# Layer 1's sliding-window scores as six single-pass products on split operands, in place of two fp32 products

## The chip, the cores and the metric

The kernel runs on one core of a Trainium2 chip, in one launch. The metric is the device time of that core in microseconds (us). TensorE is called PE here, its weight loads PEld, VectorE DVE, ScalarE ACT, GpSimd POOL, and SyncE, which issues most DMAs, SP.

## The reference, cut to what matters

A two-layer trunk over 1024 tokens of width 1024, all in float32. Layer 0 mixes by retention and by dilated attention, layer 1 by sliding-window attention with 16 query heads, 4 key heads and one sink logit per head; each layer ends in a squared-ReLU MLP of width 4096. The change touches layer 1's scores alone:

```python
def swa_mixer(h, positions, w_qkv, b_qkv, w_out, q_gain, k_gain, sinks):
    ...
    q = rope(rmsnorm(to_heads(q, SWA_Q_HEADS), q_gain), positions, ROPE_DIMS, ROPE_THETA)
    k = rope(rmsnorm(to_heads(k, SWA_KV_HEADS), k_gain), positions, ROPE_DIMS, ROPE_THETA)
    ...
    o, _ = banded_attn(q, k, v, SWA_WINDOW - 1, sinks.reshape(SWA_KV_HEADS, g))
    ...
# banded_attn, window 128, heads of 64
s = jnp.einsum('bhgnqd,bhnkd->bhgnqk', qb, kb) * (d ** -0.5)
...
p = jnp.exp(s - m)
...
o = jnp.einsum('bhgnqk,bhnkd->bhgnqd', p, vb) / den
```

## The kernel before, in words

Activations lie transposed in SBUF as two tensors each, a rounded part and a remainder (`hT_hi`, `hT_lo`), both of the type float32r, and so do the weights (`W_hi`, `W_lo`). A product of the big matrices is three single-pass products: hi with hi, hi with lo, lo with hi (`three`, lines 350 to 352). The attention's own products are in plain float32, which the chip runs as two instructions for each product.

Layer 1's attention is a software pipeline of 36 slots, written out by hand for each engine (`s_slots`). There are four groups of heads, each with one key head and four query heads, and eight blocks of 128 tokens (a = 0 to 7) in a group, so 32 slots carry a projection of one block (8 steps of three products with 384 columns, line 350). A slot has two halves (j = 0 and 1), and each half handles one unit: two of the four query heads for one block. For unit n of a half, PE does in this order: two steps of the projection; the scores of unit n (line 405); the transposes of the probabilities of unit n-1 (line 422); one step; the product with V of unit n-2 (line 434); one step. At the end of the second half PE transposes the normed queries and keys of the next block into the PSUM tile `qt` (line 441). There is one `qt`.

The other engines follow the same slots in an order of their own. ACT: squares of the queries and keys for their norms (line 652), copies `qt` out into `qT` and `kT` (lines 686, 688), copies the transposed probabilities out (line 664), takes the exponentials of a unit (lines 676, 679), and in four of each eight slots rounds a piece of the next weights (line 620). DVE: adds the bias to the projection, which frees its PSUM tile (line 1105), scales a finished unit by its denominator (lines 1071 to 1075), sums the squares (line 1006), masks the scores and finds their maxima (lines 1049 to 1057), norms and rotates queries and keys (lines 1015 to 1032). POOL: gain (line 1225), the reciprocal root (lines 1239, 1241), and the remainder of the weights' piece (line 1209). The key transposes serve both row halves: `heads_T` writes two query heads one under the other (64 partitions each) and the key head twice, so that the scores of one head use rows 0 to 63 of PE's array and those of the other rows 64 to 127. The two heads' scores go to two PSUM banks.

What holds the order together are counting semaphores: `qkt_ready` tells PE that `qT` and `kT` of a block are written, `s_done` tells DVE of finished scores, `sm_ready` tells ACT and PE that the maxima are found, `p_ready` that the exponentials are, `qt_done` that `qt` is filled, `gemm_evac` that a projection's PSUM tile is free.

Of the kernel before, what the change touches and what calls it, by code (L numbers as in the profile page):

```python
# [29 lines left out]
def hybrid_trunk(nc, x_in, positions, norm_mix, norm_mlp, w_up, w_down, w_in, w_out0, gn_gain, dq_gain, dk_gain,  # L30
                 w_qkv, b_qkv, w_out1, sq_gain, sk_gain, sinks, out, x_spill):
    f32, f32r, i32 = mybir.dt.float32, mybir.dt.float32r, mybir.dt.int32
    ALU = mybir.AluOpType
    ACT = mybir.ActivationFunctionType
    AX = mybir.AxisListType

    P = 128
    S, D = x_in.shape[1], x_in.shape[2]
    T = S // P
# [3 lines left out]
    HD = 64  # L43
# [36 lines left out]
    with ctx:  # L80
# [6 lines left out]
        def sem(name):  # L87
            return ctx.enter_context(nc.semaphore(name))
# [42 lines left out]
        off = [A0]  # L131

        def at(name, shape, dt=f32):
            t = nc.alloc_sbuf_tensor_at(name, shape, dt, offset=off[0])
            off[0] += 4 * int(math.prod(shape[1:]))
            assert off[0] <= nc.sbuf_usable_end, (name, off[0])
            return t
# [2 lines left out]
        G = at("G", [P, RING, W])  # L140
        V = at("V", [P, T, 2 * HD])
        QK = at("QK", [P, 2, W])
        kT = at("kT", [P, S])
        qT = at("qT", [P, 2, 2 * P])
        Pm = at("Pm", [P, 2, 1024])
        pT = at("pT", [P, 2, 1024])
        rsT = at("rsT", [P, P])
        rR = at("rR", [HD, 2, RV])
        rsg = at("rsg", [P, 2, RV])
        re = at("re", [P, 2, RV])  # L150
        rQK = at("rQK", [P, 2, 2 * HD])
        rqT = at("rqT", [HD, 3, P])
        off[0] = A0
        a_hi, a_lo = [0, 0], [0, 0]
        a_hi[0], a_lo[0] = at("a_hi0", [P, 2, S], f32r), at("a_lo0", [P, 2, S], f32r)
# [21 lines left out]
        sc = ps("sc", [P, 1024])  # L177
        tp = ps("tp", [P, 1024])
        o_ps = ps("o_ps", [P, 512])
        qt = ps("qt", [P, 512])  # L180
# [23 lines left out]
        r_exp, r_qk, r_qt, r_qtev, r_st, r_sT, r_R, r_o, r_var, r_rstd, r_x = [  # L204
            sem(n) for n in ("r_exp", "r_qk", "r_qt", "r_qtev", "r_st", "r_sT", "r_R", "r_o", "r_var",
                             "r_rstd", "r_x")]
        h_sq, h_gain, h_ss, h_rstd, qk_ready, qt_done, qkt_ready, v_ready = [
            sem(n) for n in ("h_sq", "h_gain", "h_ss", "h_rstd", "qk_ready", "qt_done", "qkt_ready", "v_ready")]
        s_done, sm_ready, p_ready, tp_done, pt_ready, pv_done, o_evac = [
            sem(n) for n in ("s_done", "sm_ready", "p_ready", "tp_done", "pt_ready", "pv_done", "o_evac")]  # L210
        u_done, u_evac, a_sq, a_hi_done, a_ready, d_done, d_evac = [
# [133 lines left out]
        def _(pe):  # L345
            mm = nc.tensor.matmul
# [40 lines left out]
            def scores(kind, n, u0):  # L387
                g, a, j = unit(n)
                if j == 0:
                    pe.wait_ge(qkt_ready, (u0 + n) // 2 + 1)  # L390
                if u0 + n >= 1:
                    pe.wait_ge(sm_ready, u0 + n)
                if kind == "D" and n == 0 and u0 > 0:

                    pe.wait_ge(r_x, u0 // 2)
                if kind == "D":
                    r = slice(HD * j, HD * (j + 1))
                    for c in range(0, (a + 1) * P, 512):
                        e = min(c + 512, (a + 1) * P)
                        last = mm(sc[:, c:e], qT[r, a % 2, 0:P], kT[r, c:e], start=True, stop=True)  # L400
                else:
                    k0 = max(a - 1, 0) * P
                    for e in range(2):
                        r = slice(HD * e, HD * (e + 1))
                        last = mm(sc[:, e * 512:e * 512 + (a + 1) * P - k0], qT[r, a % 2, j * P:(j + 1) * P],
                                  kT[r, k0:(a + 1) * P], start=True, stop=True)
                last.then_inc(s_done, 1)

            def blocks(kind, a):
# [28 lines left out]
            def heads_T(kind, t, a0):  # L438
                pe.wait_ge(qk_ready, a0 + t + 1)
                for m in range(2 if kind == "D" else 3):  # L440
                    last = nc.tensor.transpose(qt[:, m * P:(m + 1) * P], QK[:, t % 2, m * P:(m + 1) * P], ident[:, :])
                last.then_inc(qt_done, 1)
# [169 lines left out]
        def _(act):  # L612
            A = nc.scalar.activation
# [69 lines left out]
            def heads_T_copy(kind, t, a0):  # L683
                m = 1 if kind == "D" else 2
                act.wait_ge(qt_done, a0 + t)
                A(qT[:, (t - 1) % 2, 0:m * P], qt[:, 0:m * P], ACT.Copy)
                c = (t - 1) % T * P
                A(kT[:, c:c + P], qt[:, m * P:(m + 1) * P], ACT.Copy).then_inc(qkt_ready, 1)

            def dr_slots():  # L690
                for s in range(DR_SLOTS):
# [113 lines left out]
            for h in range(RH):  # L805
# [3 lines left out]
                last = A(cdec[:, h:h + 1], dq[:, P + 2:P + 3], ACT.Exp, scale=LG[h])  # L809
# [50 lines left out]
        def _(dve):  # L860
            E = nc.vector
# [146 lines left out]
            def prep(kind, t, a0):  # L1008

                H = 4 if kind == "D" else 5  # L1010
                q = QK[:, t % 2, 0:H * HD].rearrange("p (h d) -> p h d", h=H)
                dve.wait_ge(h_gain, a0 + t + 1)
                dve.wait_ge(h_rstd, a0 + t + 1)
                rb = rstd[:, 0:H].rearrange("p (h o) -> p h o", o=1).to_broadcast([P, H, HD])
                step.did(E.tensor_tensor(q, q, rb, ALU.mult))
                A3 = ropeA[:, 0:H * 16].rearrange("p (h s d) -> p h s d", h=H, s=2)
                B3 = ropeB[:, 0:H * 16].rearrange("p (h s d) -> p h s d", h=H, s=2)
                q4 = q[:, :, 0:2 * HALF_D].rearrange("p h (s d) -> p h s d", s=2)
                cc = cosD[:, t % T, :].rearrange("p (m s d) -> p m s d", m=1, s=1).to_broadcast([P, H, 2, HALF_D])
                sn = sinD[:, t % T, :].rearrange("p (m d) -> p m d", m=1).to_broadcast([P, H, HALF_D])  # L1020
                step.wait()
                step.did(E.tensor_tensor(A3, q4, cc, ALU.mult))
                step.did(E.scalar_tensor_tensor(B3[:, :, 0, :], q4[:, :, 1, :], -1.0, sn, ALU.mult, ALU.mult))
                step.did(E.tensor_tensor(B3[:, :, 1, :], q4[:, :, 0, :], sn, ALU.mult))
                step.wait()
                if kind == "D":
                    E.tensor_tensor(q4, A3, B3, ALU.add).then_inc(qk_ready, 1)
                else:
                    step.did(E.tensor_tensor(q4, A3, B3, ALU.add))
                    step.wait()  # L1030

                    E.tensor_copy(QK[:, t % 2, 5 * HD:6 * HD], QK[:, t % 2, 4 * HD:5 * HD]).then_inc(qk_ready, 1)
# [66 lines left out]
            def bias_G(t):  # L1099
                if t - 1 >= RING:  # L1100
                    dve.wait_ge(v_ready, A_S + t - RING)
                if (t - 1) % T == 0:
# [2 lines left out]
                E.tensor_tensor(G[:, (t - 1) % RING, :], gp[:, (t - 1) % 2, 0:W], biasS[:, (t - 1) // T % 2, :],  # L1105
                                ALU.add).then_inc(gemm_evac, 1)

            def s_slots():
                units = NG * 2 * T
                for t in range(S_SLOTS):  # L1110
                    for j in range(2):
                        n = 2 * t + j - 4
                        if j == 0 and 1 <= t <= NG * T:
                            bias_G(t)
                        if 0 <= n - 3 < units:
                            outputs("S", n - 3, U_S, 0)
                        if j == 0 and 0 <= t - 1 < units // 2:
                            sums("S", t - 1, A_S)
                        if 0 <= n < units:
                            maxima("S", n, U_S, 0)  # L1120
                        if j == 0 and 0 <= t - 1 < units // 2:
                            prep("S", t - 1, A_S)

            def out_proj(n0, k, m, full):
                lo_T(0, k, 0)
# [270 lines left out]
```

## Time and profile before

| | us |
|---|---|
| three runs, median (lowest to highest) | 2614.23 (2612.29 to 2614.32) |
| the profiled execution, its own time | 2612.44 |
| its span, first to last instruction | 2610.7 |
| layer 1's score products, first to last start | 1491.0 to 1761.5 |
| mean granted TensorE clock | 0.981 of full speed |

PE is the busy engine nearly everywhere. The stage of the change is the stretch from 1480 to about 1766 us; the other engines are busier there than in most of the kernel. A timeline row gives an instruction's start and its length; PE's instructions are pipelined, so the lengths of neighbours overlap, and the pace is read from start to start. The number behind a row in brackets is how long the engine was idle ahead of it, and what ended that.

### The profile page before, as it was taken

Reading aid. Unit: us, or ns where it says so; the run is one execution under the profiler, and the core shown is the slowest. Engines: PE = TensorE matmul, PEld = TensorE weight load, DVE = VectorE, ACT = ScalarE, POOL = GpSimd, SP = SyncE. Lnnn points to the kernel's source line nnn. Section 1 sums busy time; section 2 is a strip of 40 time slices with the busy share of each in tenths; the row PEclk is TensorE's granted clock in tenths of the full one; section 3 lists DMA queues with packets and bytes.
Section 4 is the critical chain, followed back from the end, with each engine's and each line's share of the span. In section 5 each row is a group of like instructions: output and inputs, shape, how many; then the busy total and the mean of one; then the engine's idle time right before and its main releaser. Section 6 shows DMA issues by size and latency. Waiting matters only on the chain.

```text
span 2610.7 us, 34016 instructions
## 1 busy us (share of the span) xinstructions
PE 2486.2 (95%) x12520; PEld 2080.3 (80%) x12520; DVE 1075.7 (41%) x2591; ACT 739.6 (28%) x1487; POOL 806.7 (31%) x770
## 2 busy tenths in 40 slices
PE   5999999998989999999999799999989999999998
PEld 4787878787968888888887688879978888888886
DVE  7464645454323232323233566662322323232323
ACT  4424343331221212121221355552312121212220
POOL 4223132310333333333332233331133333333331
PEclk9999999998999999999999899998999999999999
DMA  3000000002211111111111200003011111111111
GB/s 115 25 25 25 25 25 25 25 19 80 69 33 49 48 48 48 48 48 48 48 48 43 89 26 25 25 25 103 31 49 49 48 48 48 48 48 48 48 48 65
DMA packets 108200, 120.20 MB, mean 46 GB/s; under 512 B 26048, under 2 KB 94144, under 8 KB 108096
## 3 DMA queue, kind: packets, MB, share of 16 engines
q1 hardware_dynamic: 100720, 103.70, 12.8%
q10 hardware_dynamic: 7376, 15.12, 1.7%
q8 instruction: 64, 1.05, 0.2%
q14 instruction: 40, 0.33, 0.0%
HBM read 110.41 MB, written 8.39 MB: 46 GB/s over the span
## 4 chain that ended last, share of the span: by engine, by line
PE 84%; DVE 8%; POOL 3%; ACT 2%; issue 2%; DMA 0%; POOLq 0%; SPq 0%; ACTq 0%; DVEq 0%
PE gp L350 11%; PE gp L352 10%; PE gp L351 10%; PE sc L350 5%; PE sc L352 4%; PE sc L351 4%; PE tp L351 4%; PE tp L352 4%; PE tp L350 4%; PE o_ps L434 4%; PE sc L400 3%; PE tp L422 2%; PE o_ps L350 2%; PE qt L350 2%; PE qt L351 2%; PE o_ps L352 2%
## 5 line engine op out<-in xcount | busy, mean ns | idle before, releaser
L1209 POOL TENSOR_TENSOR W_lo<-raw,W_hi 128x1024 fp32r<-128x1024 f32 (+2 forms) x200 | 433.7, 2183 | 704.1 <-ACT W_hi L620 704.0
L350 PE MATMUL gp<-W_hi,hT_hi 128*128 128x384 f32 (+1 forms) x1152 | 421.9, 366 | 14.8 <-POOL W_lo L1209 6.7
L352 PE MATMUL gp<-W_hi,hT_lo 128*128 128x384 f32 (+1 forms) x1152 | 384.3, 334 | 0.0
L351 PE MATMUL gp<-W_lo,hT_hi 128*128 128x384 f32 (+1 forms) x1152 | 383.9, 333 | 0.0
L620 ACT ACTIVATE W_hi<-raw 128x1024 fp32r<-128x1024 f32 (+2 forms) x200 | 186.4, 964 | 646.7 <-PE qt L352 559.0
L1148 DVE TENSOR_TENSOR r<-r 128x512 f32<-128x512 f32 x128 | 92.2, 720 | 626.8 <-ACT r L773 626.8
L1295 POOL TENSOR_TENSOR a_lo<-r,a_hi 128x512 fp32r<-128x512 f32 x128 | 166.0, 1298 | 447.5 <-ACT a_hi L775 447.5
L1155 DVE TENSOR_TENSOR X<-tp,X 128x512 f32<-128x512 f32 x256 | 176.8, 692 | 173.8 <-PE tp L352 171.7
L350 PEld LDWEIGHTS gp<-W_hi,hT_hi 128*128 128x128 f32 x1152 | 221.2, 192 | 26.9 <-issue 11.2
L351 PEld LDWEIGHTS gp<-W_lo,hT_hi 128*128 128x128 f32 x1152 | 221.6, 192 | 0.0
L352 PEld LDWEIGHTS gp<-W_hi,hT_lo 128*128 128x128 f32 x1152 | 219.9, 191 | 0.0
L350 PE MATMUL gp<-hT_hi,W_hi 128*128 128x512 f32 x512 | 201.5, 393 | 16.0 <-POOL W_lo L1209 16.0
L350 PE MATMUL tp<-W_hi,a_hi 128*128 128x512 f32 x512 | 204.1, 399 | 11.7 <-POOL W_lo L1209 11.7
L350 PE MATMUL sc<-hT_hi,W_hi 128*128 128x512 f32 x512 | 200.9, 392 | 5.3 <-DVE hT_lo L933 5.3
L351 PE MATMUL tp<-W_lo,a_hi 128*128 128x512 f32 x512 | 204.1, 399 | 0.0
L352 PE MATMUL tp<-W_hi,a_lo 128*128 128x512 f32 x512 | 203.9, 398 | 0.0
L352 PE MATMUL gp<-hT_hi,W_lo 128*128 128x512 f32 x512 | 200.4, 391 | 0.0
L352 PE MATMUL sc<-hT_hi,W_lo 128*128 128x512 f32 x512 | 200.4, 391 | 0.0
L351 PE MATMUL sc<-hT_lo,W_hi 128*128 128x512 f32 x512 | 200.2, 391 | 0.0
L351 PE MATMUL gp<-hT_lo,W_hi 128*128 128x512 f32 x512 | 200.1, 391 | 0.0
L434 PEld LDWEIGHTS o_ps<-V,pT 128*128 128x128 f32 x1056 | 138.5, 196 | 15.8 <-issue 8.7
L434 PE MATMUL o_ps<-V,pT 128*128 128x64 f32 x1056 | 136.8, 274 | 11.1 <-DVE X L1066 7.0
(187 smaller groups left out, 4083.8 us busy)
## 6 DMA issues: line engine op xcount, KB each, us to landing
raw<-in_mlp_w_up SPq DMA_DIRECT2D x64, 512.0 KB, 3.8
raw<-in_mlp_w_down SPq DMA_DIRECT2D x64, 512.0 KB, 3.2
raw<-in_hyb_w_in SPq DMA_DIRECT2D x80, 128.0 KB, 2.5
X<-in_x SPq DMA_DIRECT2D x8, 512.0 KB, 12.0
X<-in_x ACTq DMA_DIRECT2D x8, 512.0 KB, 3.2
raw<-in_swa_w_qkv SPq DMA_DIRECT2D x16, 256.0 KB, 2.7
x_spill<-X ACTq DMA_DIRECT2D x8, 512.0 KB, 2.6
X<-x_spill ACTq DMA_DIRECT2D x8, 512.0 KB, 3.3
```

The source lines that it names most:

```text
L350: mm(o, a[0], b[0], start=first, stop=False)
L351: mm(o, a[0], b[1], start=False, stop=False)
L352: return mm(o, a[1], b[0], start=False, stop=last)
L400: last = mm(sc[:, c:e], qT[r, a % 2, 0:P], kT[r, c:e], start=True, stop=True)
L422: last = nc.tensor.transpose(tp[:, to:to + P], Pm[:, j, c:c + P], ident[:, :])
L434: last = mm(o_ps[:, e * HD:(e + 1) * HD], pT[:, j, to:to + P], V[:, c, v0:v0 + HD], start=(m == 0 or bl[m - 1][3] != e), stop=(m == len(bl ...
L620: A(W_hi[:, slot, n * p:n * (p + 1)], raw[:, p % 2, 0:n], ACT.Copy).then_inc(w_hi, 1)
L1148: E.tensor_tensor(r2[:, ft, :], r2[:, ft, :], r2[:, ft, :], ALU.mult).then_inc(a_sq, 1)
L1155: E.tensor_tensor(x, d_out[(2 * i + nh) % D_BANKS], x, ALU.add).then_inc(d_evac, 1)
L1209: E.tensor_tensor(W_lo[:, slot, c], raw[:, p % 2, 0:n], W_hi[:, slot, c].bitcast(f32), ALU.subtract).then_inc(w_ready, 1)
L1295: E.tensor_tensor(a_lo[par][:, ft, r], r2[:, ft, :], a_hi[par][:, ft, r].bitcast(f32), ALU.subtract).then_inc(a_ready, 1)
```

## The change

Queries and keys of layer 1 are kept as a rounded part and a remainder, each float32r, in memory that the layer-0 tiles had. ACT writes the rounded parts `qS_hi` and `kS_hi` from `qt` where it wrote `qT` and `kT`, and signals the new semaphore `qkt_hi`. DVE gets a new function `heads_T_lo`, two subtractions that write `qS_lo` and `kS_lo`, at the end of each slot, and signals `qkt_ready`. PE's scores of a unit are six products in place of two: hi with hi, hi with lo, lo with hi, and for each of these the two heads in turn, so that neighbouring instructions lie on different row halves. The products of one head accumulate in PSUM. Layer 0 keeps its fp32 scores. The lines of the new file are some 9 to 20 higher than those of the profile.

```diff
--- before.py
+++ after.py
@@ -140,16 +140,23 @@
         G = at("G", [P, RING, W])
         V = at("V", [P, T, 2 * HD])
         QK = at("QK", [P, 2, W])
+        qk0 = off[0]
         kT = at("kT", [P, S])
         qT = at("qT", [P, 2, 2 * P])
         Pm = at("Pm", [P, 2, 1024])
         pT = at("pT", [P, 2, 1024])
+        lo0 = off[0]
         rsT = at("rsT", [P, P])
         rR = at("rR", [HD, 2, RV])
         rsg = at("rsg", [P, 2, RV])
         re = at("re", [P, 2, RV])
         rQK = at("rQK", [P, 2, 2 * HD])
         rqT = at("rqT", [HD, 3, P])
+        off[0] = qk0
+        kS_hi, qS_hi = at("kS_hi", [P, S], f32r), at("qS_hi", [P, 2, 2 * P], f32r)
+        off[0] = lo0
+        kS_lo, qS_lo = at("kS_lo", [P, S], f32r), at("qS_lo", [P, 2, 2 * P], f32r)
+        kS, qS = (kS_hi, kS_lo), (qS_hi, qS_lo)
         off[0] = A0
         a_hi, a_lo = [0, 0], [0, 0]
         a_hi[0], a_lo[0] = at("a_hi0", [P, 2, S], f32r), at("a_lo0", [P, 2, S], f32r)
@@ -204,8 +211,8 @@
         r_exp, r_qk, r_qt, r_qtev, r_st, r_sT, r_R, r_o, r_var, r_rstd, r_x = [
             sem(n) for n in ("r_exp", "r_qk", "r_qt", "r_qtev", "r_st", "r_sT", "r_R", "r_o", "r_var",
                              "r_rstd", "r_x")]
-        h_sq, h_gain, h_ss, h_rstd, qk_ready, qt_done, qkt_ready, v_ready = [
-            sem(n) for n in ("h_sq", "h_gain", "h_ss", "h_rstd", "qk_ready", "qt_done", "qkt_ready", "v_ready")]
+        h_sq, h_gain, h_ss, h_rstd, qk_ready, qt_done, qkt_hi, qkt_ready, v_ready = [
+            sem(n) for n in ("h_sq", "h_gain", "h_ss", "h_rstd", "qk_ready", "qt_done", "qkt_hi", "qkt_ready", "v_ready")]
         s_done, sm_ready, p_ready, tp_done, pt_ready, pv_done, o_evac = [
             sem(n) for n in ("s_done", "sm_ready", "p_ready", "tp_done", "pt_ready", "pv_done", "o_evac")]
         u_done, u_evac, a_sq, a_hi_done, a_ready, d_done, d_evac = [
@@ -400,10 +407,12 @@
                         last = mm(sc[:, c:e], qT[r, a % 2, 0:P], kT[r, c:e], start=True, stop=True)
                 else:
                     k0 = max(a - 1, 0) * P
-                    for e in range(2):
-                        r = slice(HD * e, HD * (e + 1))
-                        last = mm(sc[:, e * 512:e * 512 + (a + 1) * P - k0], qT[r, a % 2, j * P:(j + 1) * P],
-                                  kT[r, k0:(a + 1) * P], start=True, stop=True)
+                    for m, (q, k) in enumerate(((0, 0), (0, 1), (1, 0))):
+                        for e in range(2):
+
+                            r = slice(HD * e, HD * (e + 1))
+                            last = mm(sc[:, e * 512:e * 512 + (a + 1) * P - k0], qS[q][r, a % 2, j * P:(j + 1) * P],
+                                      kS[k][r, k0:(a + 1) * P], start=(m == 0), stop=(m == 2))
                 last.then_inc(s_done, 1)
 
             def blocks(kind, a):
@@ -683,9 +692,13 @@
             def heads_T_copy(kind, t, a0):
                 m = 1 if kind == "D" else 2
                 act.wait_ge(qt_done, a0 + t)
-                A(qT[:, (t - 1) % 2, 0:m * P], qt[:, 0:m * P], ACT.Copy)
                 c = (t - 1) % T * P
-                A(kT[:, c:c + P], qt[:, m * P:(m + 1) * P], ACT.Copy).then_inc(qkt_ready, 1)
+                if kind == "D":
+                    A(qT[:, (t - 1) % 2, 0:m * P], qt[:, 0:m * P], ACT.Copy)
+                    A(kT[:, c:c + P], qt[:, m * P:(m + 1) * P], ACT.Copy).then_inc(qkt_ready, 1)
+                else:
+                    A(qS_hi[:, (t - 1) % 2, :], qt[:, 0:m * P], ACT.Copy)
+                    A(kS_hi[:, c:c + P], qt[:, m * P:(m + 1) * P], ACT.Copy).then_inc(qkt_hi, 1)
 
             def dr_slots():
                 for s in range(DR_SLOTS):
@@ -1105,6 +1118,13 @@
                 E.tensor_tensor(G[:, (t - 1) % RING, :], gp[:, (t - 1) % 2, 0:W], biasS[:, (t - 1) // T % 2, :],
                                 ALU.add).then_inc(gemm_evac, 1)
 
+            def heads_T_lo(t):
+                dve.wait_ge(qkt_hi, t)
+                c = (t - 1) % T * P
+                E.tensor_tensor(qS_lo[:, (t - 1) % 2, :], qt[:, 0:2 * P], qS_hi[:, (t - 1) % 2, :].bitcast(f32), ALU.subtract)
+                E.tensor_tensor(kS_lo[:, c:c + P], qt[:, 2 * P:3 * P], kS_hi[:, c:c + P].bitcast(f32),
+                                ALU.subtract).then_inc(qkt_ready, 1)
+
             def s_slots():
                 units = NG * 2 * T
                 for t in range(S_SLOTS):
@@ -1120,6 +1140,8 @@
                             maxima("S", n, U_S, 0)
                         if j == 0 and 0 <= t - 1 < units // 2:
                             prep("S", t - 1, A_S)
+                        if j == 1 and 0 <= t - 1 < units // 2:
+                            heads_T_lo(t)
 
             def out_proj(n0, k, m, full):
                 lo_T(0, k, 0)
```

PE's order in one half slot, before: `L405` are the score products of the two heads (each is two instructions on the chip), between the projection (`L351`, `L352`) and the transposes of the probabilities (`L422`).

```order
L352 MATMUL gp<-W_hi,hT_lo 128x384
L405 MATMUL sc<-kT,qT 128x256 [waits sm_ready,qkt_ready]
L405 MATMUL sc<-kT,qT 128x256
L422 MATMUL tp<-ident,Pm 128x128 [waits pt_ready,p_ready]
L422 MATMUL tp<-ident,Pm 128x128 x3
```

The same place of PE in the changed kernel, where line 405 is 414, 352 is 359 and 422 is 431.

```order
L359 MATMUL gp<-W_hi,hT_lo 128x384
L414 MATMUL sc<-kS_hi,qS_hi 128x256 [waits sm_ready,qkt_ready]
L414 MATMUL sc<-kS_hi,qS_hi 128x256
L414 MATMUL sc<-kS_lo,qS_hi 128x256 x2
L414 MATMUL sc<-kS_hi,qS_lo 128x256 x2
```

The two products in fp32 became six in float32r, two for each pair of parts; the waits of the first one are the same two.

DVE's order across the end of a slot, before: the maxima of the second half (`L1049` to `L1057`), and then the bias of the next slot (`L1105`).

```order
L1049 ISA Pm,st<-sc,c 128x256 [waits tp_done,s_done]
L1049 ISA st 128x1
L1049 ISA Pm,st<-sc,c 128x256
L1049 ISA st 128x1
L1055 TENSOR_TENSOR st<-st 128x2 [waits dve_step]
L1057 TENSOR_TENSOR st<-st 128x2 [waits dve_step]
L1105 TENSOR_TENSOR G<-gp,nlm 128x384 [waits gemm_done,v_ready]
L1071 TENSOR_TENSOR st<-st 128x2 [waits pv_done]
```

The same place in the changed kernel, where line 1049 is 1062, 1055 and 1057 are 1068 and 1070, 1105 is 1118, 1071 is 1084, and 1124 and 1125 are the new subtractions.

```order
L1062 ISA st 128x1
L1068 TENSOR_TENSOR st<-st 128x2 [waits dve_step]
L1070 TENSOR_TENSOR st<-st 128x2 [waits dve_step]
L1124 TENSOR_TENSOR qS_lo<-qt,qS_hi 128x256 [waits qkt_hi]
L1125 TENSOR_TENSOR kS_lo<-qt,kS_hi 128x128
L1118 TENSOR_TENSOR G<-gp,nlm 128x384 [waits gemm_done,v_ready]
L1084 TENSOR_TENSOR st<-st 128x2 [waits pv_done]
```

The two subtractions stand between the last maxima of a slot and the bias of the next, with a wait for ACT ahead of them.

ACT's order around the same place, before: the exponentials of the slot's second unit (`L676`, `L679`), the copies out of `qt`, and the squares of the next slot.

```order
L676 ACTIVATE st<-st 128x2 [waits sm_ready]
L679 ACTIVATE Pm,st<-Pm,st 128x256 x2
L686 ACTIVATE qT<-qt 128x256 [waits qt_done]
L688 ACTIVATE kT<-qt 128x128
L652 ACTIVATE sq<-G 128x320 [waits h_ss,gemm_evac]
```

In the changed kernel (lines 685, 688, 700, 701, 661):

```order
L685 ACTIVATE st<-st 128x2 [waits sm_ready]
L688 ACTIVATE Pm,st<-Pm,st 128x256 x2
L700 ACTIVATE qS_hi<-qt 128x256 [waits qt_done]
L701 ACTIVATE kS_hi<-qt 128x128
L661 ACTIVATE sq<-G 128x320 [waits h_ss,gemm_evac]
```

ACT's order is the same; only the tiles that it writes have other names and the type float32r.

## Rows read from the trace of the kernel before

**Rows 1.** Page of the profile, part 1: busy time and share of PE

```profile
PE 2486.2 (95%) x12520; PEld 2080.3 (80%) x12520; DVE 1075.7 (41%) x2591; ACT 739.6 (28%) x1487; POOL 806.7 (31%) x770
```

**Rows 2.** Table by stretch of layer 1's attention: window, length, busy per engine, PEclk

```profile
1500.00:1600.00 100.00, 98.93 (x666) 85.18 (x664) 67.80 (x305) 55.77 (x181) 40.70 (x53) 1.00 0.09 23
```

**Rows 3.** Chain of waits, one slot: start, length (us), piece

```profile
1602.32 0.63 PE sc L405 x4
...
1611.06 0.63 PE sc L405 x4
```

**Rows 4.** Line L405 alone, one half slot: duration ns min/median/max

```profile
L405 PE MATMUL sc<-kT,qT x4: 376/428/480, 1602.2 to 1602.6; 64*128 64x256 f32 x4
```

**Rows 5.** Timeline of PE and its weight loads in the same slot: start, length, instruction

```profile
1602.24 0.30 PEld L405 LDWEIGHTS sc<-kT,qT 64*128 64x128 f32 x4 [0.25 <-issue]
1602.25 0.70 PE L405 MATMUL sc<-kT,qT 64*128 64x256 f32 x4
...
1602.88 0.65 PE L422 MATMUL tp<-ident,Pm 128*128 128x128 f32 x4
...
1609.52 0.49 PE L441 MATMUL qt<-ident,QK 128*128 128x128 f32 x3
```

**Rows 6.** Timeline of PE, single-pass products of 256 columns (layer 0's output projection)

```profile
700.05 0.28 PE L350 MATMUL gp<-W_hi,hT_hi 128*128 128x256 f32 x1
700.17 0.28 PE L351 MATMUL gp<-W_lo,hT_hi 128*128 128x256 f32 x1
```

**Rows 7.** Timeline of DVE and ACT, the same slot

```profile
1601.05 0.56 DVE L1105 TENSOR_TENSOR G<-gp,nlm 128x384 f32<-128x384 f32 x1 [1.28 <-PE gp L352]
...
1601.74 0.47 ACT L652 ACTIVATE sq<-G 128x320 f32<-128x320 f32 x1
...
1602.36 0.49 DVE L1006 TENSOR_REDUCE st<-sq 128x5 f32<-128x320 f32 x1 [0.16 <-ACT sq L652]
...
1604.61 0.49 DVE L1015 TENSOR_TENSOR QK<-QK,st 128x320 f32<-128x320 f32 x1 [0.29 <-POOL st L1241]
...
1606.40 0.29 DVE L1075 TENSOR_TENSOR X<-o_ps,st 128x128 f32<-128x128 f32 x1
...
1607.35 0.42 DVE L1049 CUSTOM_DVE_ANT_0 Pm<-sc,c 128x256 f32<-128x256 f32 x1 [0.65 <-PE sc L405]
...
1608.36 0.16 DVE L1057 TENSOR_TENSOR st<-st 128x2 f32<-128x2 f32 x1
...
1609.56 0.19 ACT L679 ACTIVATION_READ_ACCUMULATOR Pm<-Pm,st 128x1 f32 x1
...
1610.05 0.39 ACT L686 ACTIVATE qT<-qt 128x256 f32<-128x256 f32 x1 [0.30 <-PE qt L441]
1610.33 0.27 ACT L688 ACTIVATE kT<-qt 128x128 f32<-128x128 f32 x1
```

**Rows 8.** Timeline of DVE, ACT and POOL, first two slots of a group of heads

```profile
1562.72 1.70 DVE L1032 COPY QK<-QK 128x64 f32<-128x64 f32 x1
...
1564.72 0.29 DVE L1075 TENSOR_TENSOR X<-o_ps,st 128x128 f32<-128x128 f32 x1
...
1573.39 0.71 DVE L1055 TENSOR_TENSOR st<-st 128x2 f32<-128x2 f32 x1
...
1567.18 0.39 ACT L686 ACTIVATE qT<-qt 128x256 f32<-128x256 f32 x1 [0.35 <-PE qt L441]
...
1562.47 1.90 POOL L1209 TENSOR_TENSOR W_lo<-raw,W_hi 128x768 fp32r<-128x768 f32 x1 [1.16 <-ACT W_hi L620]
...
1572.25 1.84 POOL L1209 TENSOR_TENSOR W_lo<-raw,W_hi 128x768 fp32r<-128x768 f32 x1 [1.87 <-ACT W_hi L620]
```

**Rows 9.** Timeline of PE: score products that open the group's first slots

```profile
1559.05 0.49 PE L405 MATMUL sc<-kT,qT 64*128 64x128 f32 x4
...
1568.14 0.70 PE L405 MATMUL sc<-kT,qT 64*128 64x256 f32 x4
...
1576.00 0.70 PE L405 MATMUL sc<-kT,qT 64*128 64x256 f32 x4 [0.16 <-ACT kT L688]
```

## The prediction

> **What bounds the kernel now.** I read four views, in this order. The page's first part says that PE is busy for 95% of the span [rows 1]. The table by stretch says the same of layer 1's attention: PE busy 98.9 of 100 us at full clock (1.00, the 2.4 GHz level), DVE 67.8, ACT 55.8 [rows 2]. The chain of waits shows that this is a real bound and no statistic: from one block's score products to the next, 8.74 us (1602.32 to 1611.06), every piece is PE's [rows 3]. Last I read the timeline of one such slot, for the slack of the engines that PE waits for [rows 5, 7]. PE starts the scores of a block at 1602.25 [rows 5]; ACT has the next block's keys ready at 1610.33 + 0.27 = 1610.60 [rows 7], 8.35 us later, and PE wants them at 8.74. So the slack of this hand-over is 0.39 us. That is the number on which all depends: the change puts two DVE instructions into it.
>
> **What the scores cost on PE.** One half slot has four instructions of 376 to 480 ns [rows 4], 1.71 us in sum, and yet the four take 0.70 us and the transposes start 0.63 us after the first of them [rows 5]. They run in pairs, one head on each row half. 0.63 us is made of a weight load of about 0.1, two passes of 256 columns, and 0.1 until the transposes can begin; so a pass takes some 0.213 us, two clocks for a column. In the new form there are three pairs. A float32r product of 256 columns is followed by the next after 0.12 us [rows 6], one clock for a column and a little, and its weights load behind its neighbour. Three pairs take 0.36 us against 0.43: PE gains 0.07 us in a unit, 0.13 in a slot. The ends around them (0.1 each) stay, since the array is still used in halves there and whole before and after. Bounds for a pair: 0.107 us if it is the bare columns (gain 0.11 a unit), 0.24 us if the two halves' products follow each other at the pace of [rows 6] (loss of 0.29). I take 0.12, because the fp32 pairs of this very place overlap. In units with 128 columns (8 of 64) two short passes of 0.107 stand against three pairs that a weight load of 0.1 may pace: a loss of 0.1 at most, 0.8 us in all, taken as nothing.
>
> A rule that speaks against this: the Trainium skill, "TensorE: Matmul & The Clock Gate", Part 3, The mechanism, says that weight loads overlap running products only when the row groups differ. By it, each pair would wait for its own load, and the unit would cost what the third case below has. The trace does not agree: all four loads of a unit lie within 0.30 us from 1602.24 on [rows 5], so the second pair's weights are in before the first pair has ended, on the same halves.
>
> **What the remainders cost on DVE.** Both read PSUM and SBUF, as the bias does: 0.56 us for 384 columns (L1105), 0.29 for 128 (L1075) [rows 7]. Between them 256 columns come to 0.42. On one engine the second starts some 0.07 us ahead of the first one's end, so the two take 0.36 + 0.29 = 0.65 us. Bounds: 0.5 and 0.8. ACT's copies change only the type they write, for nothing (the bounds are 0.1 us either way). DVE begins 0.15 us after ACT ends (1601.74 + 0.47 to 1602.36 [rows 7]), and PE 0.05 after what it waits for (1575.95 to 1576.00 in another slot, where PE did wait for ACT's keys [rows 9]).
>
> **The first loop, through PE.** From the scores at 0: the transposes of queries and keys at 7.27 (1609.52 - 1602.25 [rows 5]), ACT's copies from 7.80 to 8.35 [rows 7], DVE from 8.50 to 9.15, next scores at 9.20. PE's own gain shortens the first stretch by 0.13: 9.07 us, against 8.74. The added 0.85 us eats the slack of 0.39, and PE idles for the rest.
>
> **The second loop, through DVE and ACT.** DVE works in order, so behind the waiting subtraction stands the bias of the next slot; ahead of it are the maxima, whose exponentials ACT does before it copies `qt`. That closes a ring: subtraction, bias, squares (ACT), sums, root (POOL), norm, scaling, maxima, exponentials (ACT), copies (ACT), subtraction. Its length from the bias at 0, from [rows 7]: squares end at 0.62 + 0.47 and the sums start at 1.24. The norm starts 2.25 after that (1602.36 to 1604.61), 3.49; the scaling 1.79 later (1604.61 to 1606.40), 5.28; the maxima follow at once, 0.21 later, and are done after 1.17 (1607.35 to 1608.52), 6.66. Exponentials: ACT's last instruction starts 1.04 after L1057 ends (1608.52 to 1609.56), and the copies about 0.1 after that, 7.80; they end 0.55 later, DVE comes 0.15 behind, 8.50; two subtractions, 0.6 until the bias can start: 9.10 us. Before, this ring was open: DVE took the bias at 1601.05, ahead of ACT's copies. The two loops tie, and where they lean on each other a little more is lost. I take 9.15 for a plain slot: +0.4.
>
> **The slots with a weights' piece.** Four of eight slots have POOL's L1209, 1.8 to 1.9 us. While it runs, some DVE instructions stand still: the copy L1032 took 1.70 us and ended with it (1562.47 + 1.90), and L1055 took 0.71 and did so too (1572.25 + 1.84) [rows 8]. L1057, of the same kind and size as L1055, takes 0.16 [rows 7]. In most slots these stalls do not meet now, or fall in DVE's idle time; in a ring they count. In the ring's time the first maxima start at 1.67 (the sums at 1.24 and 0.43), end at 2.84, and ACT's exponentials at 3.97; the rounding of weights takes 0.83, so L1209 runs from 4.9 to 6.75, and L1055 of the second half wants 5.49 + 0.80 = 6.29: 0.46 us more, a slot of 9.55. The three slots after a group's first are such. The first one (128 columns, a shorter chain) has L1209 from 4.4 to 6.3; L1032 wants 4.8 and leaves at 6.3; the scaling ends 0.6 later at 6.9. From its end to ACT's copies are 2.17 us now (1565.01 to 1567.18 [rows 8]; PE's product with V, then the transposes), and then 1.40 (0.55, 0.15, 0.65, 0.05) to the next scores: 10.4 us.
>
> The Trainium skill, "SBUF — State Buffer", Who interferes with whom, says that GpSimd and a DVE copy, or a DVE operation with both inputs in SBUF, exclude each other for a whole instruction. The stalls above agree. By it the new subtractions, with one input in PSUM, are not held up, and the sum stays as it is.
>
> **The sum.** A group of eight slots: first 10.4 against 9.09 (1559.05 to 1568.14), second 9.55 against 7.86 (to 1576.00) [rows 9], two at 9.55 and four at 9.15 against 8.74 [rows 3]: 1.3 + 1.7 + 1.6 + 1.6 = 6.2 us. Four groups: 24.8 us. Filling and emptying the pipeline adds one or two hand-overs of 0.85 and loses a slot's worth elsewhere; I leave it at 25. The profiled execution took 2612.4 us, 1.7 of them outside its span of 2610.7, and would take 2637.4. The median of the runs lies 1.8 above it; half of that is noise of three runs, so I say 2638.5.
>
> **The rivals.**
>
> *PE's price alone decides.* DVE is idle for a third of the stage [rows 2], so the subtractions could disappear there. Then the kernel gets the 0.07 us of 56 units: 4 us faster, 0.15%, which is no change as far as this kernel can be measured (0.2%, 5 us, is about the bound). 2610. It decides as soon as the subtractions are done within 0.39 us after ACT's copies; they need 0.85. Against it: the row above, and DVE's idle time lies elsewhere, ahead of the bias and the maxima.
>
> *The ring closes, but POOL's instruction is not met.* First slot 9.1, all others 9.1 to 9.15: 0 + 1.3 + 6 x 0.4 = 3.7 a group, 15 us: 2629. For it: a shift of 0.3 us lets L1055 pass. Against: L1032 in the first slot is met in each of the four groups already, by a row like the first of [rows 8].
>
> *The six products are slower than three pairs of 0.12.* One after another, or each pair behind its own loads, a pair costs 0.21 to 0.24, a unit 0.28 to 0.36 more than in my sum. With 0.21 the PE loop becomes 9.07 + 0.54 = 9.6 us: plain slots +0.9, the middle ones no less, 2 + 4 x 0.9 + 2 x 0.9 + 1.3 = 8.7 a group: 35 us, 2648. With 0.24, 2652. This is also how the change would fail to do what it says. For it: no float32r product on half the rows is in the trace. Against: fp32 overlaps there [rows 4].
>
> **How the numbers follow.** My forecast 0.64, with its own range of 2631 to 2645; the slower products 0.15; no meeting with POOL 0.16; PE's price alone 0.05. The range of eight in ten runs from 2625, which takes in most of the 2629 case, to 2650, which takes in the 35 us case but not its end. Slower by over 0.2% is all but the last case: 0.94; within 0.2% 0.04; faster 0.02.
>
> **What would show it.** Right: in plain slots the starts of the score products stand 9.1 to 9.2 us apart; PE's largest wait in the stage is for `kS_lo` of DVE, some 0.4 us in each slot; DVE's wait for ACT's `kS_hi` becomes its longest, about 2 us in each slot, and its wait of 1.28 us for the projection is gone; ACT's squares wait for the bias; a unit's six products take about 0.6 us with starts in pairs; PE's busy share of the stage falls to some 93%. Wrong: starts of neighbouring score products 0.1 us or more apart everywhere; or PE never waits for DVE there; or L1055 is never longer than 0.2 us; or a granted clock under 1.00 in the stage, which I do not expect of gaps that short.

## The result, and the profile after

Four runs of the changed kernel have a median of 2649.78 us (2649.03 to 2650.53), the kernel before 2613.26 us in the same comparison: ratio 1.0141, 95% interval 1.0128 to 1.0153. The change costs 36.5 us. I had forecast slower, by 25 us to 2638.5; the measured time lies at the very end of my range, and outside the 2631 to 2645 of the case that I held likeliest. As a ratio to the kernel before of its own comparison it lies just past that end: 2650 is 1.0137 of the 2614.23 that I started from, and 1.0141 was measured. The mechanism was there, and one of its terms was about a third of what it should have been.

The page of the changed kernel, span and part 1 (busy time, share, instructions):

```profile
span 2647.6 us, 34336 instructions
PE 2497.7 (94%) x12648; PEld 2094.1 (79%) x12648; DVE 1102.9 (42%) x2655; ACT 739.9 (28%) x1487; POOL 805.7 (30%) x770
```

The span grew by 36.9 us, PE's recorded busy time by 11.5. Between the opening score products of the first and the last unit of layer 1 it grew by 35.8 us (269.9 us before, 305.8 now), ahead of them by 1.5, and behind them it shrank by 0.5.

The same table by stretch as in [rows 2]: window, length, busy time of PE, PEld, DVE, ACT and POOL, granted clock.

```profile
1500.00:1600.00 100.00, 88.39 (x610) 75.85 (x609) 68.93 (x277) 49.81 (x163) 35.05 (x46) 0.98 0.10 26
1600.00:1700.00 100.00, 91.27 (x636) 78.74 (x635) 68.66 (x288) 49.61 (x158) 34.29 (x48) 0.98 0.10 27
```

PE was busy 98.9 us of 100; now it idles for 9 to 12. The waits of the stage in the changed kernel, longest sums first (engine and line waited for, us in total, times, longest):

```profile
POOL QK L1247 <- DVE G L1118: 164.2, 31, 6.4
ACT st L685 <- DVE st L1070: 64.9, 60, 2.9
DVE qS_lo L1124 <- ACT kS_hi L701: 58.2, 32, 2.3
...
ACT sq L661 <- DVE G L1118: 35.7, 31, 1.2
...
PEld sc L414 <- DVE kS_lo L1125: 22.1, 31, 1.7
...
PE o_ps L443 <- DVE X L1088: 18.4, 14, 1.6
PE sc L414 <- DVE kS_lo L1125: 12.1, 30, 1.4
```

DVE waits in all 32 slots for ACT's copies, ACT's squares wait for DVE's bias, and PE waits at the scores in 30 of 32 (12.1 us; its weight loads, PEld, show the same wait as 22.1). Another wait of PE is longer in sum than the one at the scores, 18.4 us in 14 slots, for the scaling of a finished unit (L1088). What that is, the two kinds of slot show.

A plain slot, timeline of the changed kernel (start, length, instruction, idle time ahead and what ended it); these rows answer to [rows 5, 7]:

```profile
1637.46 0.27 ACT L701 ACTIVATE kS_hi<-qt 128x128 fp32r<-128x128 f32 x1
1637.77 0.42 DVE L1124 TENSOR_TENSOR qS_lo<-qt,qS_hi 128x256 fp32r<-128x256 f32 x1 [1.91 <-ACT kS_hi L701]
1638.11 0.28 DVE L1125 TENSOR_TENSOR kS_lo<-qt,kS_hi 128x128 fp32r<-128x128 f32 x1
1638.31 0.55 DVE L1118 TENSOR_TENSOR G<-gp,nlm 128x384 f32<-128x384 f32 x1
1638.89 0.47 ACT L661 ACTIVATE sq<-G 128x320 f32<-128x320 f32 x1 [1.15 <-DVE G L1118]
...
1629.39 0.39 PE L414 MATMUL sc<-kS_hi,qS_hi 64*128 64x256 f32 x2 [0.25 <-DVE kS_lo L1125]
...
1638.45 0.39 PE L414 MATMUL sc<-kS_hi,qS_hi 64*128 64x256 f32 x2 [0.25 <-DVE kS_lo L1125]
1638.67 0.28 PE L414 MATMUL sc<-kS_lo,qS_hi 64*128 64x256 f32 x2
1638.79 0.28 PE L414 MATMUL sc<-kS_hi,qS_lo 64*128 64x256 f32 x2
```

Here the forecast's sum can be read off piece by piece: DVE starts 0.04 us after ACT's copy ends (I had 0.15), the remainders take 0.42 and 0.28 (0.42 and 0.29), PE's scores start 0.06 after them, and the slot is 9.06 us long (1629.39 to 1638.45; I had 9.15, before 8.74). The three pairs start 0.22 and 0.12 us apart: the 0.12 of [rows 6] for a pair, and ahead of the second one the 0.1 that I had taken for a weight load.

A slot with a weights' piece, the same kernel, PE, DVE and POOL:

```profile
1590.35 0.39 PE L414 MATMUL sc<-kS_hi,qS_hi 64*128 64x256 f32 x2 [0.71 <-DVE kS_lo L1125]
...
1597.52 1.08 PE L443 MATMUL o_ps<-V,pT 128*128 128x64 f32 x8 [1.15 <-DVE X L1088]
1600.81 0.39 PE L414 MATMUL sc<-kS_hi,qS_hi 64*128 64x256 f32 x2 [0.26 <-DVE kS_lo L1125]
...
1594.95 0.19 DVE L1045 COPY QK<-QK 128x64 f32<-128x64 f32 x1
1595.06 1.79 DVE L1084 TENSOR_TENSOR st<-st 128x2 f32<-128x2 f32 x1
...
1597.08 0.29 DVE L1088 TENSOR_TENSOR X<-o_ps,st 128x128 f32<-128x128 f32 x1
...
1598.09 0.16 DVE L1068 TENSOR_TENSOR st<-st 128x2 f32<-128x2 f32 x1
...
1595.01 1.82 POOL L1231 TENSOR_TENSOR W_lo<-raw,W_hi 128x768 fp32r<-128x768 f32 x1 [1.47 <-ACT W_hi L629]
```

This slot is 10.46 us long, and so are eight of the twelve second, third and fourth slots of the four groups (the others 9.41 to 11.45); I had 9.55. The instruction that stands still is L1084 (before: L1071), which adds the sink to a unit's denominator: two columns wide, usually 0.15 us, here 1.79. It started 0.05 us after POOL's 1.82 us instruction. The copy ahead of it got through, and the one that I had expected to be held up, L1068, came when POOL was done. Behind L1084 stands the scaling L1088, and for that PE's product with V waits 1.15 us.

In the kernel before the same two instructions meet too, in the third slot of each group, and there DVE is not held up. One of these places (L1071 is now L1084, L1209 is now L1231, L1075 is now L1088):

```profile
1580.11 1.85 POOL L1209 TENSOR_TENSOR W_lo<-raw,W_hi 128x768 fp32r<-128x768 f32 x1 [1.52 <-ACT W_hi L620]
1580.11 0.15 DVE L1071 TENSOR_TENSOR st<-st 128x2 f32<-128x2 f32 x1
...
1580.50 0.29 DVE L1075 TENSOR_TENSOR X<-o_ps,st 128x128 f32<-128x128 f32 x1
```

With the two starts within 0.01 us of each other, L1071 takes its usual 0.15 us; with POOL 0.05 us ahead it takes 1.79. So the price of these slots hangs on 0.05 us in the order of two engines.

### The profile page after: what moved, and what is told of

Read it like the earlier page. It is cut to its first block, busy times and chain, and to the rows that moved or that the text cites. A ratio compares the mean times of both kernels' runs of the same rounds, so it can differ in the third digit from the quotient of the medians.

```text
span 2647.6 us, 34336 instructions
## 1 busy us (share of the span) xinstructions
PE 2497.7 (94%) x12648; PEld 2094.1 (79%) x12648; DVE 1102.9 (42%) x2655; ACT 739.9 (28%) x1487; POOL 805.7 (30%) x770
## 4 chain that ended last, share of the span: by engine, by line
PE 80%; DVE 11%; POOL 3%; issue 3%; ACT 2%; DMA 0%; POOLq 0%; ACTq 0%; DVEq 0%; SPq 0%
PE gp L357 10%; PE gp L359 9%; PE gp L358 9%; PE sc L357 4%; PE sc L359 4%; PE sc L358 4%; PE tp L358 4%; PE tp L357 4%; PE tp L359 4%; PE o_ps L443 4%; PE sc L407 3%; PE qt L357 2%; PE o_ps L357 2%; PE qt L358 2%; PE o_ps L359 2%
## 5 line engine op out<-in xcount | busy, mean ns | idle before, releaser
L1231 POOL TENSOR_TENSOR W_lo<-raw,W_hi 128x1024 fp32r<-128x1024 f32 (+2 forms) x200 | 432.8, 2178 | 704.4 <-ACT W_hi L629 704.3
## 6 DMA issues: line engine op xcount, KB each, us to landing
X<-in_x SPq DMA_DIRECT2D x8, 512.0 KB, 11.5
```

The lines of the kernel that those rows point to most:

```text
L1231: E.tensor_tensor(W_lo[:, slot, c], raw[:, p % 2, 0:n], W_hi[:, slot, c].bitcast(f32), ALU.subtract).then_inc(w_ready, 1)
```

## The experiments

Each comparison has its own runs of the kernel before; times are medians. "Remainders" are the two subtractions L1124 and L1125.

**POOL's long instruction taken away.** The stall was a reading of one trace, so first the cause is removed.

```diff
-                        split_lo(P_S + 4 * (t // T + 1), SPLIT_AT[t % T], t // T % 2, 2 * W)
+                        split_lo(P_S + 4 * (t // T + 1), SPLIT_AT[t % T], t // T % 2, 2 * W, 16)   # 16 columns only
```

> The changed kernel, but POOL computes the weights' remainder for 16 of 768 columns of each piece in layer 1's attention (the rest is left out), so its long instruction is gone there. Theory A (the four slots of a group with a weights' piece are long because DVE stands still while that instruction runs): these slots fall from 10.4 to about 9.1 us, plain slots stay at 9.06, the kernel gets 4 x (1.3 + 3 x 1.4) = 22 us faster than the changed one, about 2628 us. Theory B (those slots are long because the new ring of DVE and ACT also has the rounding of weights in it): they stay near 10.4, and the time near 2650 us.

2625.24 us (2623.14 to 2626.89), a little under the 2628 expected. The third and fourth slots of a group are 9.05 to 9.09 (one 9.22), like the plain ones; the first two are 8.8 and 8.9 (7.9 for the very first). In the trace of this run the score products of the former long slots start at:

```profile
1591.69 0.39 PE L414 MATMUL sc<-kS_hi,qS_hi 64*128 64x256 f32 x2 [0.25 <-DVE kS_lo L1125]
...
1600.76 0.39 PE L414 MATMUL sc<-kS_hi,qS_hi 64*128 64x256 f32 x2 [0.25 <-DVE kS_lo L1125]
...
1609.83 0.39 PE L414 MATMUL sc<-kS_hi,qS_hi 64*128 64x256 f32 x2 [0.25 <-DVE kS_lo L1125]
```

9.07 us each. Theory A holds; the rounding of weights on ACT, which is still there, costs nothing.

**The six products without remainders.**

```diff
-        kS, qS = (kS_hi, kS_lo), (qS_hi, qS_lo)
+        kS, qS = (kS_hi, kS_hi), (qS_hi, qS_hi)
-                    A(kS_hi[:, c:c + P], qt[:, m * P:(m + 1) * P], ACT.Copy).then_inc(qkt_hi, 1)
+                    A(kS_hi[:, c:c + P], qt[:, m * P:(m + 1) * P], ACT.Copy).then_inc(qkt_ready, 1)
```

> The six products as in the changed kernel, but the rounded parts stand in for the remainders (these are left out): DVE's two subtractions are gone, and ACT signals the scores as before. This is PE's price alone. Theory A: six products take 0.55 us until the transposes where the fp32 ones took 0.63, so the stage gains 0.15 us a slot: 4 to 5 us faster than the kernel before, about 2609 us. Theory C (the products themselves are the loss): 2640 us or more.

2612.48 us, ratio 1.0000 (0.9990 to 1.0009): no loss, and no gain of 4 us either. Plain slots are 8.59 us, 0.16 shorter as forecast. But the third slot of each group is 9.53 where it was 8.75. DVE and POOL in it:

```profile
1580.64 1.79 DVE L1084 TENSOR_TENSOR st<-st 128x2 f32<-128x2 f32 x1
...
1583.10 1.08 PE L443 MATMUL o_ps<-V,pT 128*128 128x64 f32 x8 [0.71 <-DVE X L1088]
...
1580.58 1.83 POOL L1229 TENSOR_TENSOR W_lo<-raw,W_hi 128x768 fp32r<-128x768 f32 x1 [1.46 <-ACT W_hi L629]
```

L1084 comes 0.06 us behind POOL's start, where in the kernel before the two started together and it passed. A faster PE shifted two engines against each other by 0.06 us, and one such meeting in each group eats all but 0.1 us of what PE won in the other slots (69.33 us a group against 69.45).

**Both at once: PE's price with nothing in its way.** The two edits above together, and POOL's cut alone in the kernel before.

> The six products with the rounded parts in the remainders' place and no subtraction (the remainders are left out), and POOL's instruction on the weights cut to 16 columns. PE's price with nothing in its way: each slot 0.15 us shorter than in the kernel before with the same cut (2607.3 us), 8.60 where that has 8.75, so about 4.5 us less, 2603 us. If the six products bring nothing on the whole, 2607 us.

> The kernel before, with POOL's remainder of the weights cut to 16 of 768 columns of each piece in layer 1's attention (the rest is left out). Before, the stalls behind POOL's long instruction meet only the first two slots of a group: 1 us there, 4 to 6 us in all, about 2608 us. Set against the same cut in the changed kernel (2625 us) this gives what the change costs with POOL out of the way: theory A says 17 us, and that 20 of the 36 us are stalls that the old order did not meet.

2605.13 us (ratio 0.9964, 0.9950 to 0.9978) against 2607.30 (0.9978, 0.9969 to 0.9988). The times alone don't tell the two apart; the slots do. Score products of two neighbouring plain slots, first kernel and then second:

```profile
1599.62 0.62 PE L414 MATMUL sc<-kS_hi,qS_hi 64*128 64x256 f32 x6
...
1608.21 0.62 PE L414 MATMUL sc<-kS_hi,qS_hi 64*128 64x256 f32 x6
```

```profile
1600.10 0.70 PE L405 MATMUL sc<-kT,qT 64*128 64x256 f32 x4
...
1608.85 0.70 PE L405 MATMUL sc<-kT,qT 64*128 64x256 f32 x4
```

8.59 against 8.75. Over the stage, 261.0 against 264.5 us: the six products gain 3.5 us, near my 4. The second run says more: with POOL's instruction gone, the change costs 2625.24 - 2607.30 = 17.9 us, so of the 36.3 us between the kernels the stalls behind it are about 18 (I had expected 20).

**The remainders without the products.** Two fp32 products as before, and the subtractions at their place, with the waits of the changed kernel.

```diff
+                        if j == 1 and 0 <= t - 1 < units // 2:
+                            heads_T_lo(t)      # results unused; scores from qT and kT, L405 as it was
```

> The kernel before with its two fp32 products, plus the two subtractions of the changed kernel at the same place and with the same waits (their results are not used). Theory A: the loss is the subtractions' place, so this kernel has all of it and lacks PE's small gain: plain slots about 9.2, long ones about 10.4, 2650 to 2655 us. Theory C: near the kernel before, 2613 us.

2648.68 us (ratio 1.0135, 1.0118 to 1.0152), which is the changed kernel's time within the noise. Plain slots 9.15, long ones 10.46. With the runs on PE's price this settles it: the loss is the subtractions, and the products are innocent.

**Does the place on DVE matter?** The same subtractions, behind the bias of the next slot.

```diff
                         if j == 0 and 1 <= t <= NG * T:
                             bias_G(t)
+                        if j == 0 and 0 <= t - 2 < units // 2:
+                            heads_T_lo(t - 1)
...
-                        if j == 1 and 0 <= t - 1 < units // 2:
-                            heads_T_lo(t)
```

> The changed kernel with the two subtractions moved behind the bias of the next slot on DVE, nothing else. Theory A: the ring through the bias is open again, so POOL's root and the norms come 0.5 us or more earlier and the stalls behind POOL's instruction are partly met elsewhere; plain slots stay at 9.05 to 9.2, since PE still waits for the remainders; long slots fall to 9 to 10. Between 2632 and 2643 us. A rival (it is DVE's added work of 0.65 us a slot, wherever it stands) expects no change, 2650 us.

2632.07 us (ratio 1.0072, 1.0055 to 1.0089): half of the loss is gone with the same work on DVE. Timeline of this kernel, DVE and ACT at the hand-over:

```profile
1637.04 0.56 DVE L1118 TENSOR_TENSOR G<-gp,nlm 128x384 f32<-128x384 f32 x1 [1.29 <-PE gp L359]
1637.29 0.38 ACT L700 ACTIVATE qS_hi<-qt 128x256 fp32r<-128x256 f32 x1 [0.32 <-PE qt L450]
1637.87 0.42 DVE L1124 TENSOR_TENSOR qS_lo<-qt,qS_hi 128x256 fp32r<-128x256 f32 x1 [0.28 <-ACT kS_hi L701]
```

The bias waits for PE alone again (1.29 us, 1.28 in [rows 7]), and the ring is open. ACT's copies wait for PE's transposes again (0.32 us), which they did not in the changed kernel. Plain slots went to 8.90, less than I expected: that is the loop through PE alone, and 0.16 of their 9.06 had been the ring. Slots with a piece are 9.85, and in eleven of the twelve second to fourth slots of a group L1084 still takes 1.8 us. The rival, that it is the work wherever it stands, falls.

**And the wait at the scores?** On top of that, PE does three steps of the projection ahead of a slot's first scores, not two.

```diff
-                        next(steps)
-                        next(steps)
+                        for _ in range(3 - j):
+                            next(steps)
...
                             trans("S", n - 1, U_S)
-                        next(steps)
+                        if j == 1:
+                            next(steps)
```

> The subtractions behind the bias (as in the run before with that move), and on PE the first unit's scores come after three steps of the projection in place of two, which gives the remainders 0.52 us more. Theory A: PE no longer waits for them, plain slots fall from 8.9 to 8.6 us, and PE is the bound again there; slots with a weights' piece stay near 9.3 to 9.8 because of POOL. About 2621 us. If the wait at the scores were not the bound of plain slots, they stay at 8.9 and the time at 2632 us.

2624.05 us (ratio 1.0043, 1.0026 to 1.0060), 3 us more than expected. Plain slots are 8.63 us, and PE's products wait for the remainders in 7 slots where they did in all 32 of the run before. What is left stands in the slots with a piece: the first of a group is 9.85, the third 10.03.

```profile
PE o_ps L443 <- DVE X L1089: 10.5, 9, 1.5
PE sc L414 <- DVE kS_lo L1126: 6.8, 7, 1.6
```

**The stall made short and not removed.** POOL's instruction as four of 192 columns: first on top of the last kernel, then in the changed kernel alone.

```diff
+                w = n // parts
+                for i in range(parts):
+                    c = slice(p * n + i * w, p * n + (i + 1) * w)
+                    last = E.tensor_tensor(W_lo[:, slot, c], raw[:, p % 2, i * w:(i + 1) * w],
+                                           W_hi[:, slot, c].bitcast(f32), ALU.subtract)
+                last.then_inc(w_ready, 1)
```

> As the run with three steps, and POOL computes each weights' piece as four instructions of 192 columns (about 0.5 us each) instead of one of 1.8 us; all is computed. Theory A: a DVE instruction stands still for at most 0.5 us at a time, two or three times a slot; slots with a piece fall from about 9.7 to 8.9 to 9.2, so 2611 to 2616 us. If a stall lasts until all four are done (the next one takes the port at once), no change against three steps alone.

> The changed kernel with POOL's weights' piece as four instructions of 192 columns in layer 1's attention, all computed. Theory A: the stalls of 1.3 to 1.8 us become 0.3 to 0.8, slots with a piece fall from 10.46 to 9.3 to 9.8, plain ones stay at 9.06: 2633 to 2640 us. The rival that a long slot is the ring's own length expects 2650 us.

2615.44 us (1.0009, 0.9999 to 1.0019) and 2635.19 us (1.0081, 1.0063 to 1.0100). In the first kernel:

```profile
1580.80 0.56 DVE L1085 TENSOR_TENSOR st<-st 128x2 f32<-128x2 f32 x1
...
1582.60 0.41 DVE L1069 TENSOR_TENSOR st<-st 128x2 f32<-128x2 f32 x1
...
1580.75 2.24 POOL L1234 TENSOR_TENSOR W_lo<-raw,W_hi 128x192 fp32r<-128x192 f32 x4 [1.46 <-ACT W_hi L630]
```

DVE gets in between two of POOL's pieces: these two instructions last 0.56 and 0.41 us, where L1084 alone had lasted 1.79; the longest one held up in the first kernel is an addition of 80 columns, 0.67 us. In the changed kernel long slots fell from 10.46 to 9.49, its plain ones stayed at 9.06, so the rival that a long slot is the ring's own length falls. With all three helps (2615.44 us) the six products do no better than the kernel before (2613.52 in the same comparison).

**Are the turns needed?** The three products of the first head, then the three of the second.

```diff
-                    for m, (q, k) in enumerate(((0, 0), (0, 1), (1, 0))):
-                        for e in range(2):
+                    for e in range(2):
+                        for m, (q, k) in enumerate(((0, 0), (0, 1), (1, 0))):
```

> The changed kernel with the six products in another order: the three of the first head, then the three of the second, so that neighbours lie on the same rows of the array. If the two halves overlap only when they are issued in turns, the six take 6 x 0.12 + 0.1 = 0.8 us until the transposes, 0.3 more than in turns; since PE is in the loop through the remainders with the first and the second unit of a slot, plain slots grow from 9.06 to 9.5 to 9.6 us and the kernel by 10 to 15 us, to about 2662 us. If the order does not matter (the array overlaps them anyway, or did not overlap them in turns either): 2650 us.

2649.66 us, as the changed kernel. The timeline shows the first two products in one merged row and the next two 0.22 us later, just as in turns:

```profile
1601.73 0.39 PE L414 MATMUL sc<-kS_hi,qS_hi 64*128 64x256 f32 x2 [0.26 <-DVE kS_lo L1125]
1601.95 0.28 PE L414 MATMUL sc<-kS_lo,qS_hi 64*128 64x256 f32 x2
```

The transposes follow 0.555 us after the first product, 0.55 in turns. The order within these six makes no difference here. Whether the array or something ahead of it pairs them was not tried.

**What beats both kernels.** The two helps in the kernel before, with its fp32 scores: pieces alone, and with the three steps.

> The kernel before, with POOL's weights' piece as four instructions of 192 columns in layer 1's attention, all computed. The stalls meet only the first two slots of a group there: these fall by 0.5 to 1 us together in each of four groups, 2 to 4 us in all, about 2610 us.

> The kernel before with the same four pieces on POOL and the first unit's scores behind three steps of the projection. PE had 0.39 us of slack for the keys and gains nothing in plain slots (8.75, perhaps 8.65 for one mode change less beside the transposes); in the first slot of a group the later scores lie behind the copies, so 0.5 us less. About 2608 us, and 2610 if the step does nothing.

2608.82 us (ratio 0.9986, 0.9977 to 0.9995) and 2609.66 us (0.9982, 0.9973 to 0.9991). Both are faster than the kernel before (2612.57) by 3 to 5 us, and the two can't be told apart, though the stage is 266.9 and 264.2 us long in their traces. Plain slots are 8.75 and 8.74: PE bounds them, and the third step brings nothing there, as expected.

## Why the prediction was right, and where it was wrong

Sign and mechanism were right, the size was short: 25 us forecast, 36.5 measured. The step that failed is the stall behind POOL's instruction in the three slots after a group's first, put at 0.46 us on L1055; it was 1.64 us on L1084.

- *PE's price* (0.13 us a slot): 0.16 measured, 8.59 for 8.75. *That it decides* had 5%; with the subtractions gone but POOL's instruction whole no gain reached the time, because one stall moved.
- *The two loops of a plain slot* (9.07 and 9.10, taken as 9.15): 9.06. I had called them a tie. With the ring opened the slot is 8.90, so the loop through PE was 0.17 too long in my sum, 0.11 of it in DVE's start after ACT (0.04 and not 0.15), and the ring decides these slots.
- *The first slot of a group* (10.4; its terms, 6.9, 2.17 and 1.40, add up to 10.47): 10.36 in three groups and 9.36 in the first, though not by the instruction I named. I had named the copy L1032 (now L1045); in the changed kernel L1042, the addition just ahead of it, takes 1.78 us and ends within 0.1 us of POOL's. That the number came out is in part luck.
- *The three slots after it* (9.55): 10.46, the step that failed. I wrote that L1055 "of the second half wants 5.49 + 0.80 = 6.29: 0.46 us more". I had listed only the two instructions that my rows showed standing still, and not every one of the same kind. L1084 (before L1071) also has both inputs in SBUF. In the slot of [rows 7] it starts 1.40 us after the norm L1015 (1606.01 against 1604.61), so my own ring times put it at 3.49 + 1.40 = 4.9, beside POOL's 4.9:

```profile
1606.01 0.15 DVE L1071 TENSOR_TENSOR st<-st 128x2 f32<-128x2 f32 x1
```

With it the stall is 1.64 us (1.79 less the usual 0.15), not 0.46, and the slot is 1.40 us longer than a plain one. These slots lose 0.91 us more than forecast in three of eight, 2.7 a group, 11 us in all; the plain ones give back 0.4 a group. The Trainium skill, "SBUF — State Buffer", Who interferes with whom, which I had quoted, names a DVE operation with both inputs in SBUF as such. The trace agrees, 1.79 us beside POOL's 1.82, and the rule applied to each row of DVE's order would have found L1084.
- The sum over a group in the trace: 10.36 + 3 x 10.46 + 4 x 9.06 = 78.0 us against 69.4 before, 8.5 for my 6.2; four such groups are 34 of the 36.9 us of the span. The rest of the miss lies at the ends, which I had left at nothing: the first score product came 1.5 us later, and the last group, up to its last unit, grew by 1.3 more than the two ahead of it. In its last 14 us, from 1785 us, the granted clock was 0.56 where the same end had 0.75 before.

Of the signs that I named, DVE's wait of 2 us (1.91 in the slot above), ACT's squares behind the bias and the pairs came as said. Four did not quite: plain slots are 9.06 us and not 9.1 to 9.2; PE's products wait longer in sum for L1088 (18.4 us) than for `kS_lo` (12.1); PE's busy share fell to 88 to 91%, not 93; and the granted clock was 0.98 over the two stretches and not 1.00. The clock fell in two places, in both behind waits of PE for the scaling L1088 (1.59 us up to 1509.09, and 1.61 and 1.51 us up to 1665.03 and 1675.83):

```profile
1508.00:1516.00 8.00, 6.91 (x40) 6.24 (x41) 5.30 (x23) 3.65 (x13) 2.81 (x5) 0.79 0.19 51
1668.00:1680.00 12.00, 10.17 (x65) 8.70 (x67) 8.69 (x34) 5.65 (x17) 4.52 (x6) 0.90 0.12 35
```

The slot of the second place took 11.45 us where its neighbours take 10.46, but the one behind it took 9.41: L1084 came 0.25 us ahead of POOL's instruction there and was not held up. The group has 77.93 us, like the one ahead of it with 77.97, so this drop cost nothing in the end. Why the clock fell here and not behind a wait of 1.61 us at 1587.06 stays open.

## What to carry to other kernels

Before you add a step between two engines, look up how long its input lies ready ahead of its use (0.39 us here) and what stands behind the waiting instruction on its engine: a wait for the last work of a slot, placed ahead of the first work of the next, closes a ring, here through DVE, ACT and POOL. Moving the same two instructions by one place gave back 18 of 36 us. Whether a stall is met can turn on 0.05 us between two starts, so list every instruction that can meet the long one, and make the long one short rather than rely on the timing.

## What the runs showed of the hardware that I had not expected

A two-column addition on DVE stood still for 1.79 us because POOL had begun a subtraction of 768 columns 0.05 us earlier, and took its usual 0.15 us where the two started within 0.01 us of each other. With four pieces of 192 columns no DVE instruction that was held up lasted over 0.67 us, at a cost to POOL of 2.24 us in place of 1.8. And products on two row halves overlapped in pairs whether or not their order in the program took turns (0.55 us for the six either way).
